# A hybrid SSD and S5 decoder block on one core: the z and x projections computed with the weights as the moving operand, and the gate stage's x brought to tokens through DRAM

## What is computed

```
hn = rmsnorm(h, norm_mix_w)
z, xbc, dt_raw, u, g_a, g_b = split(hn @ w_in)      # z 3072, x 3072, b 1024, c 1024, dt 48, u 1024, gates 4096
xbc = silu(causal_dwconv(xbc, conv_w, conv_b))      # 4 taps along the tokens, per channel
xs, bm, cm = split(xbc)
dt  = softplus(dt_raw + dt_bias)                    # one factor per token and head, 48 heads of 64 channels
cb     = einsum("ln,sn->ls", cm_g, bm_g)            # for each of 8 groups of 6 heads
y      = einsum("ls,rls,srp->lrp", cb, exp(segsum(A*dt)), xs*dt) + d_skip*xs
y      = rmsnorm_per_group(y * silu(z)) * norm_w;  y_a = y @ w_proj
y_b    = S5 mixer on u (64 groups, 64 complex states each, scanned along the tokens)
h      = h + (sigmoid(g_a)*y_a + sigmoid(g_b)*y_b) @ w_out
h      = h + conv-gated MLP(rmsnorm(h));  out = rmsnorm(h)
```

## Time and profile before

| | |
|---|---|
| runs | 1680.24, 1680.87, 1680.90 us |
| profiled execution | 1680.3 us, span of the core 1678.6 us |
| granted TensorE clock | 0.998 of full speed |
| stages in the trace, about | u to 59, zx to 343, bc to 441, gate to 640, the rest to 1678 us |
| PE / DVE / ACT / POOL busy | 1667.1 / 1320.3 / 962.7 / 216.4 us |
| DMA | 358.5 MB, mean 214 GB/s |

### The profile page before, as it was taken

One profiled execution on the slowest core, in us unless ns is written; L12 is line 12 of the kernel. 1 busy time (PEld: TensorE's weight loads), 2 busy tenths in 40 slices (PEclk: granted clock), 3 DMA queues, 4 the chain that ended last, 5 costly groups with the idle time before them and its releaser, 6 DMA issues.

```text
span 1678.6 us, 24422 instructions
## 1 busy us (share of the span) xinstructions
PE 1667.1 (99%) x8340; PEld 1395.1 (83%) x8340; DVE 1320.3 (79%) x1685; ACT 962.7 (57%) x1271; POOL 216.4 (13%) x310
## 2 busy tenths in 40 slices
PE   9999999999999999999999999999999999999997
PEld 8888888888788888888888888888888888888886
DVE  7999999999998986545775868888878888845555
ACT  7676676766666667444557755444444444454553
POOL 7843342221000000000000200000000000000001
PEclk9999999999999999999999999999999999999999
DMA  7666766666666566656786577777777777666653
GB/s 254 213 197 199 204 206 200 193 188 190 194 217 231 191 219 189 199 191 201 239 254 232 174 233 241 243 241 244 242 244 241 245 232 248 225 194 195 191 189 123
DMA packets 174569, 358.49 MB, mean 214 GB/s; under 512 B 16880, under 2 KB 39584, under 8 KB 174368
## 3 DMA queue, kind: packets, MB, share of 16 engines
q1 hardware_dynamic: 162528, 338.26, 62.5%
q0 software_dynamic: 11248, 18.37, 4.6%
q10 hardware_dynamic: 720, 0.93, 0.2%
HBM read 335.41 MB, written 15.80 MB: 209 GB/s over the span
## 4 chain that ended last, share of the span: by engine, by line
PE 73%; DVE 2%; issue 0%; ACT 0%; DVEq 0%
PE psum L1822 22%; PE psum L1823 22%; PE psum L1824 22%; PE psum L1783 3%; PE psum L1785 2%; PE psum L1908 1%; DVE wlo L1107 0%; PE psum L1909 0%; DVE vn L1749 0%; PE psum L1933 0%; DVE bc L1303 0%; PE psum L1829 0%; PE psum L1924 0%; DVE dec L1416 0%; PE psum L1982 0%; PE psum L1979 0%
## 5 line engine op out<-in xcount | busy, mean ns | idle before, releaser
L1107 DVE TENSOR_TENSOR wlo<-raw,whi 128x1024 fp32r<-128x1024 f32 x580 | 709.6, 1230 | 321.3 <-ACT whi L666 314.0
L666 ACT ACTIVATE whi<-raw 128x1024 fp32r<-128x1024 f32 x580 | 611.9, 1058 | 577.1 <-PE psum L1824 455.1
L1783 PE MATMUL psum<-act,whi 128*128 128x512 f32 x1088 | 342.5, 396 | 0.0
L1822 PE MATMUL psum<-whi,nw 128*128 128x512 f32 x704 | 274.1, 389 | 0.0
L1824 PE MATMUL psum<-whi,nw 128*128 128x512 f32 x704 | 273.9, 389 | 0.0
L1823 PE MATMUL psum<-wlo,nw 128*128 128x512 f32 x704 | 273.9, 389 | 0.0
L1785 PEld LDWEIGHTS psum<-act,wlo 128*128 128x128 f32 x1088 | 204.4, 188 | 48.3
L1785 PE MATMUL psum<-act,wlo 128*128 128x256 f32 x1088 | 213.7, 278 | 0.0
L1783 PEld LDWEIGHTS psum<-act,whi 128*128 128x128 f32 x1088 | 165.6, 189 | 3.3 <-issue 2.8
L1824 PEld LDWEIGHTS psum<-whi,nw 128*128 128x128 f32 x704 | 132.1, 188 | 27.6
L1822 PEld LDWEIGHTS psum<-whi,nw 128*128 128x128 f32 x704 | 132.1, 188 | 27.3
(11 more groups left out here) (251 smaller groups left out, 2300.3 us busy)
## 6 DMA issues: line engine op xcount, KB each, us to landing
raw<-in_w_up SPq DMA_DIRECT2D x176, 512.0 KB, 4.9
raw<-in_w_zx SPq DMA_DIRECT2D x96, 512.0 KB, 3.7
raw<-in_w_down SPq DMA_DIRECT2D x88, 512.0 KB, 3.8
raw<-in_w_gate SPq DMA_DIRECT2D x64, 512.0 KB, 5.6
raw<-in_w_proj SPq DMA_DIRECT2D x48, 512.0 KB, 4.4
raw<-in_w_bc SPq DMA_DIRECT2D x32, 512.0 KB, 3.7
raw<-in_w_glu SPq DMA_DIRECT2D x32, 512.0 KB, 4.4
raw<-in_w_out SPq DMA_DIRECT2D x32, 512.0 KB, 4.8
```

What stands on the lines that cost most here:

```text
L666: fn(whi[:, s, :], raw[:, s, :], ACTF.Copy).then_inc(hi_ready, 1)
L1107: V.tensor_tensor(wlo[:, s, :], raw[:, s, :], whi[:, s, :], ALU.subtract).then_inc(lo_ready, 1)
L1783: mm(psum[:, b + t, :], whi[:, s, cols(t)], x, start=first, stop=False)
L1822: mm(banks[:, t, :], x_hi, high[:, k], start=j == 0 and k == 0, stop=False)
```

## The change

The zx stage is computed with `unit_tokens`, in 12 chunks of eight units; chunk c holds the z and the x of tiles 2c and 2c+1. ACT rearranges the sums (`zx_blocks`), SP writes and fetches them through DRAM (`zx_write`, `zx_fetch`, behind loads 2, 3, 10 and 11 of a turn), DVE turns the blocks of z into `zblk` and those of x into `cpad` (`zx_turned_back`, four transposes for each chunk), and the convolution of a chunk stands one to two groups later than before, so that the last two chunks are convolved in the first bc turn. The additions of the two halves are gone for zx.

In the gate stage PE's transposes and DVE's product with dt are gone, and so is the copy `xst`. DVE turns x of the group in 32x32 blocks (`x_turned`), POOL writes them to DRAM in four DMAs and fetches them in one (`token_write`, `token_fetch`), and ACT multiplies with dt in twelve activations of 128x64 (`tokens`). For the first group SP moves the blocks in the same way, in the bc stage, ahead of the gate stage (`first_tokens_write`, `first_tokens_fetch`). DVE still copies dt (`dtt`, L1431) in the first gate turn, now ahead of `cbm`, and ACT's `tokens` of the first group wait for it. PE waits for the result (`xtok_ready`) ahead of `heads(0)`. On DVE, `tokens` shrinks to the product for `cbm`. The product for `cbm` reads b directly, without the copy `bst`.

```diff
+            def zx_write(c):
+
+                sp.wait_ge(zx_free, c + 1)
+                for q in range(4):
+                    sp.dma_start(blocks_at[:, :, q, :].rearrange("j p x -> p j x"),
+                                 flat_x[32 * q:32 * q + 32, :, :, :, :].rearrange("p j s t b -> p j (s t b)")
+                                 ).then_inc(zx_written, 16)
+
+            def zx_fetch(c):
+
+                sp.wait_ge(zx_written, c * 64 + 64)
+                sp.dma_start(quad_x[:, :, :, :, :].rearrange("p q s t b -> p (q s t b)"),
+                             blocks_at.rearrange("j p q x -> (j p) (q x)")).then_inc(zx_read, 16)
+
+            def zx_moves(turn, j):
+
+                if j % 8 == 2:
+                    zx_write(turn * 2 + (j // 8 - 2))
+                if j % 8 == 3:
+                    zx_fetch(turn * 2 + (j // 8 - 2))
...
+            def token_write(g):
+
+                pool.wait_ge(x_blocks, g + 1)
+                for a in range(4):
+                    pool.dma_start(tokens_at[g % 2, :, :, a, :].rearrange("q j x -> j q x"),
+                                   xblk[g][32 * a:32 * a + 32, :, :, :, :].rearrange("j q k t i -> j q (k t i)")
+                                   ).then_inc(x_written, 16)
+
+            def token_fetch(g):
+
+                pool.wait_ge(x_written, 64 * g)
+                if g > 1:
+                    pool.wait_ge(xtok_ready, g)
+                pool.dma_start(xraw[g][:, :, :, :, :].rearrange("p a k t i -> p (a k t i)"),
+                               tokens_at[g % 2].rearrange("q j a x -> (q j) (a x)")).then_inc(x_read, 16)
+
+            for i in range(GROUPS - 1):
+                token_write(i + 1)
                 for half in range(2):
                     pool.wait_ge(y_ready, i * 2 + (half + 1))
                     load_decay(i + 1, half)
+                token_fetch(i + 1)
...
+            def zx_blocks(c, cc):
+
+                act.wait_ge(unit_used, c * 8 + (UNIT0["zx"] + 8))
+                if not (isinstance(c, int) and c == 0):
+                    act.wait_ge(zx_written, c * 64)
+                for t in range(2):
+                    ins = fn(flat_x[:, :, :, t, :].rearrange("p j s b -> p s j b"),
+                             chunk_banks("zx", cc)[:, t, :].rearrange("p (s j b) -> p s j b", s=4, j=4), ACTF.Copy)
+                ins.then_inc(zx_free, 1)
+
+            def x_first_tap(c):
+
+                act.wait_ge(zx_turned, c + 1)
+                act.nop(nofuse=True)
+                pad = last_pad if isinstance(c, int) and c == 11 else cpad
+                for t in range(2):
+                    q = c * 2 + t
+                    ins = fn(zx[:, ds(q, 1), 1, :].rearrange("p o n -> p (o n)"), pad[:, t, 3:3 + L], ACTF.Identity,
+                             scale=col("conv_a_w", q * 4 + 3), bias=col("conv_a_b", q))
+                ins.then_inc(x_tap, 1)
+
+            def x_silu(c):
+
+                act.wait_ge(x_conv, c + 1)
+                act.nop(nofuse=True)
+                to = zx[:, ds(c * 2, 2), 1, :]
+                fn(to, to, ACTF.Silu).then_inc(xbc_done, 1)
+
+            def z_silu(c):
+
+                fn(zx[:, ds(c * 2, 2), 0, :], zblk[:, :, :], ACTF.Silu).then_inc(z_done, 1)
...
-                def stage(g):
-                    fn(bst[:, :], bc[:, ds(g, 1), 0, :].rearrange("p o n -> p (o n)"), ACTF.Copy).then_inc(staged, 1)
-                    fn(xst[:, :, :], zx[:, ds(g * TPG, TPG), 1, :], ACTF.Copy).then_inc(staged, 1)
+                def tokens(g, k):
+
+                    act.wait_ge(x_read if g else first_read, 16 * max(g, 1))
+                    for hd in range(HPG):
+                        a = hd % 2 * 2
+                        ins = fn(xtok[:, k, 64 * hd:64 * hd + 64].rearrange("p (a i) -> p a i", a=2),
+                                 xraw[g][:, a:a + 2, k, hd // 2, :], ACTF.Identity,
+                                 scale=dtt[:, k, g * HPG + hd:g * HPG + hd + 1])
+                    if k == 1:
+                        ins.then_inc(xtok_ready, 1)
 
                 if prev is None:
...
                 fn(zx[:, ds(i * TPG, TPG), 0, :], zx[:, ds(i * TPG, TPG), 1, :], ACTF.Square).then_inc(ysq_ready, 1)
                 hi(7)
+                if not last:
+                    tokens(i + 1, 0)
+                    tokens(i + 1, 1)
 
                 act.wait_ge(unit_used, u0 + 8)
...
+            def zx_turned_back(c):
+
+                pad = cpad
+                dve.wait_ge(zx_read, c * 16 + 16)
+                if isinstance(c, int) and c == 11:
+                    pad = last_pad
+                    V.memset(pad[:, :, 0:3], 0.0).then_inc(pad_zeros, 1)
+                if not (isinstance(c, int) and c == 0):
+                    dve.wait_ge(z_done, c)
+                for t in range(2):
+                    V.transpose(zblk[:, :, t * P:t * P + P].rearrange("p s (q b) -> p q s b", q=4),
+                                quad_x[:, :, 0:2, t, :])
+                if not (isinstance(c, int) and c == 0):
+                    dve.wait_ge(x_conv, c)
+                for t in range(2):
+                    ins = V.transpose(pad[:, :, 3 + t * P:3 + t * P + P].rearrange("p s (q b) -> p q s b", q=4),
+                                      quad_x[:, :, 2:4, t, :])
+                ins.then_inc(zx_turned, 1)
+
+            def x_conv_pair(c):
+
+                dve.wait_ge(x_tap, c + 1)
+                to = [zx[:, ds(c * 2 + t, 1), 1, :].rearrange("p o n -> p (o n)") for t in range(2)]
+                pad = cpad
+                if isinstance(c, int) and c == 11:
+                    dve.wait_ge(pad_zeros, 1)
+                    pad = last_pad
+                conv_pair(to, c * 2, 4, "conv_a_w", "conv_a_b", x_conv, True, frm=pad)
...
                     lo(3)
 
             s5_fractions(1)
...
+            def x_turned(g):
+
+                if g == 0:
+                    dve.wait_ge(xbc_done, 2)
+                elif g == 1:
+                    dve.wait_ge(y5_ready, 8)
+                elif g == GROUPS - 1:
+                    dve.wait_ge(xbc_done, 12)
+                if g > 1:
+                    dve.wait_ge(x_written, 64 * (g - 1))
+                for k in range(2):
+                    ins = V.transpose(xblk[g][:, :, k, :, :].rearrange("p q t i -> p t q i"),
+                                      zx[:, TPG * g:TPG * g + TPG, 1, k * P:k * P + P]
+                                      .rearrange("p t (q i) -> p t q i", q=4))
+                ins.then_inc(x_blocks, 1)
+
+            x_turned(0)
             mixer_turn("bc", 0, 6, ("zx", 5, 3))
...
                     blocks(0)
                     blocks(1)
                     if not first_scan:
                         lo(1)
+                    if i < GROUPS - 1:
+                        x_turned(i + 1)
                     lo(2)
                     group_norm(prev)
                     lo(3)
                     group_lo(prev)
                 lo(4)
+                if prev is None:
+                    x_turned(1)
                 lo(5)
...
+            def zx_turn(i, prev):
+
+                for c in range(2):
+                    for j in range(8):
+                        if prev is None and c == 0:
+                            pe.wait_ge(vlo_ready, j // 2 + 1)
+                        if prev is not None and c == 1 and j == 0:
+                            pe.wait_ge(y5_out, prev + 1)
+                        unit_tokens("zx", c, j, act16, i)
+                        if c == 0 and j == (0 if prev is None else 1):
+                            s5_drive(i, prev is None)
+                            if prev is not None:
+                                pe.wait_ge(zx_free, i * 2)
+                                s5_products(prev, YS5)
...
                 def heads(half):
                     pe.wait_ge(m_ready, i * 2 + (half + 1))
+                    if half == 0:
+                        pe.wait_ge(xtok_ready, i + 1)
                     for k in range(HALF):
                         hd = half * HALF + k
```

236 lines of the change are left out of this document (133 added, 103 removed).

## The result

The changed kernel takes 1730.6 us, median of 4 runs (1728.1 to 1732.2), against 1680.7 us before: a ratio of 1.030, 95% interval 1.028 to 1.031. Forecast were 1692.7 us in a range of 1682 to 1708. The direction was right, and 38 us of the size were missing.

A forecast was written before the change was run, and what follows sets the result against it. The prediction took PE as the bound, with DVE nearly full in zx and bc. Its terms, -6.5 + 4.0 + 13.8 + 0.5 = +11.8 us on 1680.3, plus 0.6 for the median, gave 1692.7 us, range 1682 to 1708.

The forecast's parts named there:

- I take no wait: zx stage: DVE's ten own instructions cover each chunk's way through DRAM, so no waiting was counted.
- the fourth rival: zx stage: DVE waits 1 us for each chunk's fetch, twelve waits less 5 us of slack; 1699 us, chance 0.05.
- ACT's rearranging takes the place of the four copies of halves, about even.: zx stage, ACT: rearranging the sums costs about what the dropped copies of halves cost, so no time was counted.
- PE in zx, -6.5 us: zx stage: each of 96 units takes 2.720 us of PE instead of 2.788, giving 6.5 us less.
- the first bc turn, +4.0 us: First bc turn: DVE, the bound there, gets a convolution, chunk 11's transposes and x_turned(0), about 4.0 us more.
- the prediction's last part: Expected profile after: zx turns of 45.8 us, PE waiting about 4 us for the state sum, later gate turns 26 to 27.
- Gate turn 1, 9.2 us: Gate turn 1: fetched x blocks reach ACT late behind writes and decay loads, so heads(0) come 9.2 us late.
- The small activations: Gate stage, ACT: twelve activations of 64 elements that multiply with dt, 0.25 us each, 3.0 us a turn.
- the 1 us for the place in the queue: Gate turn 1: the fetch, queued behind 1.2 MB of decay loads, lands 1 us after them.
- The closed loop, 26.6 us: Gate turns 2 to 7: round trip of 12.7 us plus following work of 13.9 us sets each turn at 26.6 us.
- the first rival: Gate stage: block moves share DMA engines with weight loads, making the loop 28.5 us; 1704 us, chance 0.22.
- The faster rival, 8 x 0.65 us off the end: Gate stage: blocks arrive before ACT needs them, so removed PE transposes save 0.65 us a turn; 1673 us, chance 0.09.

The follow-up runs named there:

- zg_old: Changed kernel with both zx repairs (Silu table loaded ahead, block writes and fetch issued earlier) and the old gate stage put back: 1677.83 us, ratio 0.998.
- z_tables: Changed kernel with a Silu of one column added ahead of the zx stage, so the function table is loaded before the loop: 1723.35 us, ratio 1.026.
- z_moves: Changed kernel with SP issuing each zx chunk's block writes two units earlier and the fetch one unit earlier: 1717.23 us, ratio 1.022.
- zg_early_late: Changed kernel with both zx repairs, x moved a gate turn ahead, ACT's scaled copies before unit 6, block writes held until the last unit's use: 1678.74 us.
- zg_dve_late: Changed kernel with both zx repairs, x moved a gate turn ahead, dt's factor on DVE, block writes held until the last unit's use: 1679.38 us.
- g_ahead: Changed kernel with x's way to tokens one gate turn ahead, and POOL's fetch issued before decay loads and writes: 1712.91 us, ratio 1.019.

## Why the prediction was wrong, step by step

**"I take no wait" for the way of zx through DRAM.** This step failed, by 13.4 us, the costliest of the zx stage. The prediction took the way as short enough for DVE's ten instructions, and left out that SP may issue the fetch only when the four writes have landed: it stood there 36.4 us in ten waits, up to 5.0 us each. So the fetch was late for DVE, which waited 9.3 us for it in ten waits. That is the fourth rival's mechanism nearly to its price (1 us for each fetch), but its 7 us came short: it let 0.9 us of slack in each turn cover a part, and in each of these turns DVE also waited 2 us for `tab`. That the second used up the first is argued, not shown. Late weights, which no rival of the zx stage names, were the smaller part here: 1.9 us of DVE's waits are for `whi`, and zg_old runs at full pace with 22.5 us of ACT's waits for weights. With the table loads gone they weigh more: of DVE's 12.4 us of waits in z_tables 5.2 are for `quad_x` and 3.4 for `whi`, and both go when the moves are repaired too. Of the 12.6 us that z_moves gains at the first heads, DVE's waits account for 11.0; the rest is open.

**"ACT's rearranging takes the place of the four copies of halves, about even."** Failed by 7.2 us. The activations themselves are even; the table loads are not. Three of them in each of five turns are 19 us of ACT, of which 7.2 reached PE, through DVE's wait for the sine table and PE's for the rearranged sums. The Trainium skill (ScalarE: Activation LUTs, What ACT_TABLE_LOAD costs) gives about 1283 ns for the load and about 1380 ns of drain with it. The trace agrees with the first (1.28 us) and shows nothing of the second: the next activation starts 1.29 us after the load. With the whole of it the loads would be 40 us of ACT, an estimate from that page. The Trainium skill (ScalarE activation tables: per-element evaluation and per-set limits, Table sets in the compiler and the runtime) says that loads are placed block by block, which fits a load at the head of a loop that the rest of the turn has no need of.

**PE in zx, -6.5 us, and the first bc turn, +4.0 us.** Right. Without those waits a turn takes 45.82 us (45.8 forecast) and the gate stage starts 2.15 us earlier (2.5 forecast). PE's wait for the state sum is 2.26 us; the prediction's last part said about 4, which was too much.

**Gate turn 1, 9.2 us.** The mechanism was right and mis-sized: 13.6 us. The prediction has 10.5 us from the end of `x_turned(1)` to the landed fetch; the trace has 14.7 (481.33 to 496.06). The missing term is POOL's wait for the four writes to land, 3.31 us, with which the fetch is issued 4.4 us behind the first decay load and not right behind the second. The small activations (0.25 us apart forecast, 2.97 us for twelve measured) and the 1 us for the place in the queue stand.

**The closed loop, 26.6 us.** Measured 28.5 us, the length that the first rival had taken. That was luck in part: its reason, block moves that share the DMA engines with weight loads, is priced at 2.7 us for the whole stage by zg_early_late and 5.1 by zg_dve_late, not at the 11 us that the rival adds to the forecast. The two halves of the turn of 27.7 us that ends at 567.6 us: 13.8 us from `x_turned` to the small activations (12.7 forecast) and 13.9 us from there on (13.9 forecast). But the first half is not only the way through DRAM. ACT's wait there is for gate weights, which land late among decays and block writes (2.67 us for unit 7). And g_ahead, which takes the round trip out, still has turns of 26.9 us. What sets the turn is the later of two, the round trip or a weight load, and behind it the small activations, `gates`, split and DVE's scans. Why a gate weight load on that chain takes so long to land (8.8 to 11.0 us here, 6.4 to 9.7 in g_ahead) is open but for the part of the writes. Three runs price the parts: the round trip 17.7 us with turn 1's stall, the small activations behind it 10.2, the writes in the crowd 2.7. Together that is 30.6 of the 30.9 us, though the last price is from a kernel with the repaired zx stage.

**The faster rival, 8 x 0.65 us off the end.** It had the transposes' time come off a turn of 26.0 us. In zg_dve_late a turn falls to 25.6 us on average, three of the five to 25.3 or 25.4 as the rival has it, and the bc stage takes the gain back: by its median the kernel is 1.6 us behind zg_old, not 5.2 us ahead. That PE has no gap in a turn of 26.0 us did not mean that PE alone sets it.

The sum as it should have stood, from the profiled execution's 1680.3 us: -6.5 + 4.0 + 13.4 + 7.2 + 13.6 + 15.7 = +47.4 us. Measured is 50.3; of the rest, 1.4 us stand ahead of the first heads, about what the two zx repairs give together beyond their sum (21.9 against 20.6), and 1.5 behind the last ones, which no run explains. The total landed outside the range because the waits of zx stood at nothing (20.6 us) and the gate stage's 29.3 us at 13.8; the range had been made from the landing times of decay loads and the price of the small activations alone.

## What to carry to other kernels

A round trip through DRAM costs two landings one after the other, since the fetch is issued only when the writes have landed, and it holds all that stands behind the fetch on its queue. Price it on the engine that sets the pace: here that was DVE, and 39.3 us of ACT's waits for weights reached it as 1.9 us, beside 9.3 us of its own for the blocks. Issue such a fetch one or two steps behind the point where its writes have surely landed, and let the writes go when no other burst moves. On ACT, count table loads for each turn of a loop: if the loop's last function is one that the code ahead of the loop hasn't used, the head of the loop may load again in every turn, and one dummy activation takes that away.

## What the hardware showed beside that

- Twelve activations of 128x64 with a column as scale take 333 ns each and start 0.24 us apart; two of 384 elements take 598 ns each, so six times the width takes 1.8 times as long. The Trainium skill (ScalarE: Activation LUTs, What ACT_TABLE_LOAD costs) has 186 ns plus 0.833 ns an element, about 93 ns for a column operand and as much overlap, from which I work out, as an estimate, 239 ns between two starts; the trace agrees.
- Behind its waits PE also ran slower for a while. The heads at 593.98 us start after PE had waited 2.4 us, and their products of 256 columns then come at 1.12 us for four instead of 0.65; in the stretch from 590 to 600 us the granted clock is 0.83 of full speed (1.00 in the ten us before and behind it), so a part of it is at the lower of the two levels (1.2 and 2.4 GHz). A stall costs somewhat more than its own length; how much was not measured apart.
